# Routing choices packed by expert for each tile of tokens by itself, 32 columns a tile, expert and round

## What is computed

```python
def hierarchical_moe(hn, w_router_group, w_router_expert, w_gate, w_up, w_down):
    g_probs = softmax(t @ w_router_group);  g_w, g_idx = lax.top_k(g_probs, 1)      # 4 groups
    e_in_group = (t @ w_router_expert)[group g_idx]                                  # 8 experts each
    top_l, top_i = lax.top_k(e_in_group, TOP_K_INNER)                                # 2 experts a token
    weights = softmax(top_l) * g_w
    comb = sum(one_hot(ids, N_EXPERTS) * weights[..., None], axis=1)
    for e in range(N_EXPERTS):
        hid = silu(t @ w_gate[e]) * (t @ w_up[e])                                    # 2048 -> 256
        out = out + (hid @ w_down[e]) * comb[:, e:e + 1]                             # 256 -> 2048
```

## Time and profile before

| | before |
|---|---|
| median of 3 runs | 3268.54 us (3267.64 to 3271.41) |
| span of the profiled execution | 3266.3 us |
| PE busy | 2940.1 us, 90% |
| DVE, ACT, POOL busy | 1239.7, 549.1, 697.1 us |
| DMA | 1206.82 MB, 369 GB/s over the span |

### The profile page before, as it was taken

The page is one execution under the profiler, slowest core; times in us unless marked ns, Lnnn a source line. Parts: engine busy times, 40 slices in busy tenths (PEclk is TensorE's granted clock), DMA queues, the critical chain, the costliest instruction groups (busy, mean ns, idle before and its releaser), DMA issues.

```text
span 3266.3 us, 24078 instructions
## 1 busy us (share of the span) xinstructions
PE 2940.1 (90%) x8045; PEld 1303.3 (40%) x8045; DVE 1239.7 (38%) x1913; ACT 549.1 (17%) x1298; POOL 697.1 (21%) x599
## 2 busy tenths in 40 slices
PE   8999998899999999997688788878799899999999
PEld 4444444344444444443333333333354433333344
DVE  1101004535454443345756655554522122322220
ACT  1111001112121110112213211211122111000010
POOL 1000002323234222223434434334300010000000
PEclk9999999999999999998889888998899999999999
DMA  9878888999999999999999999999977659999972
GB/s 358 300 278 288 303 302 311 416 412 412 416 416 419 421 422 421 422 421 416 412 419 406 419 419 419 419 419 419 373 278 262 238 238 422 422 422 422 422 299 78
DMA packets 268084, 1206.82 MB, mean 369 GB/s; under 512 B 16656, under 2 KB 19280, under 8 KB 164688
## 3 DMA queue, kind: packets, MB, share of 16 engines
q1 hardware_dynamic: 193600, 668.09, 52.8%
q0 software_dynamic: 74384, 537.49, 39.8%
HBM read 1203.41 MB, written 2.10 MB: 369 GB/s over the span
## 4 chain that ended last, share of the span: by engine, by line
PE 47%; DMA 40%; DVE 4%; issue 3%; DVEq 2%; ACT 1%; SPq 1%; POOL 1%; ACTq 0%; POOLq 0%
DMA W<-in_peer_expert_down,big 27%; PE bank L973 14%; DMA W<-in_w_expert_up 8%; PE bank L1545 6%; PE bank L963 5%; PE bank L1150 5%; PE bank L1652 4%; DMA W<-in_w_in 4%; PE bank L1710 3%; PE bank L1040 3%; DVEq L2471 2%; DVE W L2622 2%; PE bank L1636 1%; PE bank L1622 1%; DMA W<-in_w_peer_query 1%
## 5 line engine op out<-in xcount | busy, mean ns | idle before, releaser
L2622 DVE CUSTOM_DVE_ANT_0 W<-W,big 128x2048 f32<-128x2048 f32 x256 | 586.3, 2291 | 703.6 <-DMA W<-in_peer_expert_down,big 702.8
L901 POOL DMA_INDIRECT W<-in_peer_expert_down,big x256 | 351.8, 1374 | 1206.8 <-DVE small L2622 643.8
L1545 PE MATMUL bank<-XT,big 128*128 128x512 f32 x488 | 304.5, 782 | 206.8 <-ACT big L2002 186.4
L973 PE MATMUL bank<-W,XT 128*128 128x512 f32 x672 | 297.9, 601 | 5.3 <-DMA W<-in_w_peer_query 5.3
L1545 PEld LDWEIGHTS bank<-XT,big 128*128 128x128 f32 x488 | 119.9, 256 | 381.1 <-issue 258.4
L1545 PE MATMUL bank<-XS,big 128*128 128x512 f32 x536 | 246.3, 603 | 24.0 <-ACT big L2002 18.2
L1994 ACT ACTIVATE small<-small 128x1 f32<-128x1 f32 x256 | 51.8, 202 | 1223.0 <-DVE small L2622 1203.6
L1545 PE MATMUL bank<-W,big 128*128 128x512 f32 x512 | 235.7, 604 | 16.2 <-ACT big L2002 12.9
L1652 PE MATMUL bank<-W,XS 128*64 128x512 f32 x1024 | 226.6, 596 | 14.1 <-DMA W<-in_w_expert_up 11.4
L1150 PE MATMUL bank<-W,XT 128*128 128x512 f32 x480 | 214.9, 598 | 13.4 <-DMA W<-in_w_in 11.6
L963 PE MATMUL bank<-W,XT 128*128 128x512 f32 x480 | 211.4, 598 | 4.1 <-DMA W<-in_w_in 4.1
(11 more groups left out here) (387 smaller groups left out, 2715.4 us busy)
## 6 DMA issues: line engine op xcount, KB each, us to landing
W<-in_w_in SPq DMA_DIRECT2D x66, 2048.0 KB, 7.9
W<-in_w_in SPq DMA_DIRECT2D x132, 1024.0 KB, 12.5
W<-in_w_expert_gate SPq DMA_DIRECT2D x68, 1024.0 KB, 15.0
W<-in_w_expert_up SPq DMA_DIRECT2D x68, 1024.0 KB, 17.0
big<-in_w_expert_down SPq DMA_DIRECT2D x32, 2048.0 KB, 12.6
W<-in_w_out SPq DMA_DIRECT2D x16, 2048.0 KB, 8.1
W<-in_w_out SPq DMA_DIRECT2D x32, 1024.0 KB, 11.6
W<-in_w_peer_query SPq DMA_DIRECT2D x28, 1024.0 KB, 11.4
```

Of the source, the lines that this page charges most:

```text
L901: pool.indirect_dma_start(down_row(n), None, down_t, row).then_inc(down_in[n % DOWN_ROWS], 16)
L973: mm = pe.matmul(out, lhs(k), slot(i)[:, k, :], start=first and k == 0, stop=last and k == ks - 1)
L1545: mm = pe.matmul(bank[4 * (n // P) + c][:, :], DIAG[:, m % 4, :], up_row(n)[:, c * CH:(c + 1) * CH], start=n % P == 0, stop=n % P == P - 2)
L2622: dve.tensor_tensor_reduce(out=down_row(n), in0=down_row(n), in1=HN[n // P], scale=1.0, scalar=0.0, op0=ALU.mult, op1=ALU.add, accum_out=d ...
```

## The change

Each tile's choices are packed on their own: 256 places a tile instead of 512 for both, and 32 columns (CAPT) per tile, expert and round. An expert still has 64 columns in the loop, 32 from each tile. A further round is run if an expert has more than 32 choices in one tile.

The routing code on DVE becomes three functions called once a tile: `choose_experts`, `count_experts`, `place_choices`. For tile 0 they are steps of the table, during tile 1's output projections; for tile 1 they follow `logits(1)`. Tile 0's packing matmuls (`pack(0, ...)`) follow the table on PE, tile 1's follow those. A pair of slices k shares a bank (two times 256 columns); tile 0 uses banks 0 to 2, tile 1 banks 4 to 6. All of tile 0's pairs are moved out by ACT; of tile 1's, ACT takes the odd ones and DVE the even. `keep_scaled(1)` leaves ACT: POOL copies tile 1's columns unscaled, and the scale goes into tile 1's SELP. The index row that SELP is compared with is 256 wide and is loaded earlier. POOL copies 8 windows a pair instead of 4, each half as wide. Cut to its core:

```diff
+CAPT = CAP // T2
+MAX_ROUNDS = P // CAPT
-PACKED = 512
+PACKED = 2 * P
+            put(dve, a + 4, "experts", 0)
+            put(pe, a + 6, "rank", 0)
+            put(dve, a + 7, "places", 0)
 # SP
+            sp.dma_start(places_iota, consts[:, CONST_W:CONST_W + PACKED]).then_inc(iota_loaded, 16)
             for i in range(INDEX["in2", 1, 1, 0], UG):
                 load(i)
-            sp.dma_start(iota512, consts[:, CONST_W:CONST_W + PACKED]).then_inc(iota_loaded, 16)
 # POOL
+            for c in range(4):
+                pool.wait_ge(out2_added, 4 + c + 1)
+                pool.tensor_copy(XS[:, 1, :].rearrange("p (k d) -> p k d", k=KC)[:, :, 32 * c:32 * c + 32],
+                                 H[:, 1, c * CH:(c + 1) * CH].rearrange("p (d k) -> p k d", k=KC)).then_inc(xs_ready, 1)
...
+                        pool.wait_ge(packed_first, KC // 2)
+                        pool.wait_ge(packed_act, 2)
+                        pool.wait_ge(packed_dve, 2)
+                        for e in range(2):
+                            for t in range(T2):
+                                to = e * CAP + t * CAPT
+                                pool.tensor_copy(XTE[:, p, 0:7, to:to + CAPT], XPA[:, t, :, ds(at[e][t], CAPT)])
                         pool.wait_ge(packed_act, 4)
-                        pool.wait_ge(packed_dve, 3)
+                        pool.wait_ge(packed_dve, 4)
...
 # PE
+            def pack(t, pairs):
+                for j in pairs:
+                    if j == 0:
+                        pe.wait_ge(places_ready, t + 1)
+                        pe.wait_ge(xs_ready, 5 if t else 1)
+                        pe.wait_ge(out2_added, 7)
...
+                    if j >= 3 and t == 0:
+                        pe.wait_ge(packed_first, j - 2)
+                    elif j >= 3:
+                        pe.wait_ge(packed_dve if j % 2 else packed_act, (j - 3) // 2 + 1)
+                    for k in (2 * j, 2 * j + 1):
+                        mm = pe.matmul(pack_out(t, k), XS[:, t, k * P:(k + 1) * P], SELP[:, t, :], start=True, stop=True)
+                    mm.then_inc(packed_mm, 1)
+            pack(0, range(0, 5))
+            rank(1)
+            pack(0, range(5, KC // 2))
+            pack(1, range(KC // 2))
 # ACT
-            keep_scaled(1)
-            act.wait_ge(route_in, 1)
+            for j in range(KC // 2):
+                keep_packed(0, j, packed_first)
+            act.wait_ge(route_in, 2)
             act.activation(GEXP, GEXP, ACT.Exp)
             act.activation(RSC[:, :, 0:1], RSC[:, :, 0:1], ACT.Exp).then_inc(route_exp, 1)
-            for k in range(0, KC, 2):
-                act.wait_ge(packed_mm, k + 1)
-                act.activation(packed(k), bank[4 + k % 4][:, :], ACT.Copy, scale=GP[:, k:k + 1]).then_inc(packed_act, 1)
+            for j in range(1, KC // 2, 2):
+                keep_packed(1, j, packed_act)
 # DVE
+                    elif kind == "experts":
+                        dve.wait_ge(attended, 8)
+                        choose_experts(*what)
+                    elif kind == "places":
+                        count_experts(*what)
+                        place_choices(*what)
...
             logits(1)
+            choose_experts(1)
+            count_experts(1)
+            place_choices(1)
...
-                TS(over[:, m - 1:m], most, float(m * CAP), None, ALU.is_gt)
+                TS(over[:, m - 1:m], most, float(m * CAPT), None, ALU.is_gt)
...
-            for k in range(1, KC, 2):
-                dve.wait_ge(packed_mm, k + 1)
-                TS(packed(k), bank[4 + k % 4][:, :], GP[:, k:k + 1], None, ALU.mult).then_inc(packed_dve, 1)
+            for j in range(0, KC // 2, 2):
+                dve.wait_ge(packed_mm, KC // 2 + j + 1)
+                TT(packed_pair(2 * j), bank[4 + j % 3][:, :].rearrange("p (k s) -> p k s", k=2),
+                   GP[:, 2 * j:2 * j + 2].unsqueeze(2).to_broadcast([P, 2, PACKED]), ALU.mult).then_inc(packed_dve, 1)
```

More of the change, by code:

```diff
@@ L620, in half_of, with packed, pack_out, packed_pair @@
             return W[:, half_slot(half, e), :].rearrange("p (g n) -> p g n", g=2)
[L622 to L624 removed]
+        def packed(t, k):
+            return XPA[:, t, k, 0:PACKED] if k < 7 else XPB[:, t, k - 7, 0:PACKED]
+        def pack_out(t, k):
+            return bank[4 * t + k // 2 % 3][:, k % 2 * PACKED:(k % 2 + 1) * PACKED]
+        def packed_pair(k):
+            return XPA[:, 1, k:k + 2, 0:PACKED] if k < 7 else XPB[:, 1, k - 7:k - 5, 0:PACKED]
         def moving(half, e, k):
@@ L1532, in turn3, with rank @@
                 turn_four(turn3_out(t, c), H[:, t, c * CH:(c + 1) * CH]).then_inc(turned3, 1)
+            def rank(t):
+                pe.wait_ge(comb_ready, t + 1)
+                if t == 0:
+                    pe.wait_ge(probs_kept, 8)
+                tri = const("tri")
+                for j in range(2):
+                    mm = pe.matmul(bank[7][:, (2 * t + j) * EXPERTS:(2 * t + j + 1) * EXPERTS], tri[:, j * P:(j + 1) * P],
+                                   PICK[:, t, :], start=True, stop=True)
+                mm.then_inc(ranked, 1)
+            def pack(t, pairs):
[4 more added lines that the diff above has]
+                        pe.wait_ge(out2_added, 7)
+                        if t == 1:
+                            pe.wait_ge(kept3, 8)
+                            pe.wait_ge(logits_ready, 2)
+                    if j >= 3 and t == 0:
[5 more added lines that the diff above has]
+                    mm.then_inc(packed_mm, 1)
             pe.wait_ge(late_rows, 4 * 16)
@@ new lines, in place_choices @@
+            def place_choices(t):
+                one = [SELP[:, t, :], SELQ]
+                dve.wait_ge(iota_loaded, 16)
+                dve.drain()
+                for q in range(2):
+                    if t == 0:
+                        TS(one[q], places_iota, PLACE[:, t, q:q + 1], None, ALU.is_equal)
+                    else:
+                        TS(one[q], places_iota, PLACE[:, t, q:q + 1], rstd[:, t:t + 1], ALU.is_equal, ALU.mult)
+                dve.drain()
+                TT(one[0], one[0], one[1], ALU.add).then_inc(places_ready, 1)
```

204 lines of the change are left out of this document (93 added, 111 removed).

## The result

The changed kernel takes **3243.48 us**, the median of 4 runs (3242.88 to 3247.04). The kernel before, on the same chip, takes 3268.76 us (3267.64 to 3271.41, 4 runs). The ratio is 0.992, with a 95% interval of 0.9908 to 0.9932: faster by 25.3 us. Forecast were 3248 us and a range from 3244 to 3256.

A forecast was written before the change was run, and what follows sets the result against it. The path was held to run from router through packing to the loop's first refill; the loop starting 20.85 us earlier, less 0.45 for tile 0's ranks, gave span 3245.9, plus 2.2 to the median: 3248.1 us, range 3244 to 3256.

The forecast's parts named there:

- what bounds the kernel: Router to expert loop: 44.8 us on the path; an earlier loop start moves the first weight refill and the end.
- Rival 5: Expert loop starts earlier but ends when it did, which needs DMA busy before 2655 us; chance 0.01.
- fewer columns: Packing on PE: the same 64 records with 256 columns take 0.215 us each at full clock, instead of 0.43.
- Rival 2: Packing: each 256-column record waits for its bare weight load; gain 11.4 to 13 us, 3255.5 us or more; chance 0.03.
- tile 0's routing beside the projections: During tile 1's projections: DVE routes tile 0 with 3 us to spare; its ranks cost PE 0.45 us.
- DVE's hold: Tile 1's fourth packing pair: PE stands 2.5 us, a new wait, until DVE's first eviction.
- rival 3: Tile 1's packing: DVE holds PE under 1 us; gain near 22.5 us, 3246 us, or 3244 at full clock; chance 0.05.
- the clock term: Packing: 6 to 11 of the first 20 records at half clock, plus 1.1 us for a renewed fall after DVE's hold.
- the low bound: Whole kernel: the lower end of the predicted range, 3244 us, meant to take in the clock bounds nearly whole and rival 3.
- clock full throughout: Router to loop: DVE counts from 2606.4, later steps come 1.9 us earlier, 1.1 us vanishes; gain 23.4, time 3245.1 us.
- Rival 1: Both packings: low clock stays through most, as two waits cut PE's work; gain 11.4 to 17, 3251 to 3257 us; chance 0.12.
- Rival 4: Expert loop: over 32 choices in one tile makes all 16 pairs run again, adding 459 us, 3707 us; chance 0.02.

The follow-up runs named there:

- Six banks: Changed kernel with six PSUM banks in turn for tile 1's packing instead of three, so PE need not wait for DVE's first eviction: 3246.73 us, ratio 0.9923.
- the repetition: The changed kernel run and profiled once more with nothing changed: 3246.48 us, ratio 0.9924.
- after_filled: Changed kernel with unused matmuls of constants in PE's waits: 3242.77 us, ratio 0.9915.
- tile0_late: Changed kernel with tile 0's choosing, ranks and places moved back behind the table, narrow packing kept: 3259.14 us, ratio 0.9962.

## Why the prediction was right, and where it failed

**Right: what bounds the kernel.** The path was held to run from the router through packing to the first refill, and from there a fixed time to the end. The refill came 24.28 us earlier and the span 24.3 us; the rest of the span differs by 0.6. Rival 5 (nothing gained) falls.

**Right: fewer columns.** At full clock 12 records take 2.86 us and 20 take 4.58, so each further one costs 0.215 us, the value forecast. Every one of them has a weight load of its own, about 0.2 us long:

```profile
2615.98 4.18 PEld L1583 LDWEIGHTS bank<-big,XS 128*128 128x128 f32 x20 [2.37 <-DVE XT L2873]
```

The rule of the Trainium skill (TensorE: Matmul & The Clock Gate, section The mechanism), that a weight load overlaps a matmul only on other rows of the array, would make that near 0.4 us by these rows; the trace disagrees, and the measurement decides. Another section of the same page of the Trainium skill (Step-by-step: what each phase is for) also lets a load into the background weight buffer run ahead, and with that the trace agrees. Rival 2 falls. The narrow packing is worth 12.7 us at full clock.

**Right: tile 0's routing beside the projections.** DVE had 3.87 us left before its next addition, where I expected 3. With the ranks, PE comes from U to the next transposes in 34.78 us instead of 34.33, so they cost 0.45 (forecast 0.45). POOL's scattered copies took 1.05 us each, not 0.6. That costs nothing, since the cover would have held four times 0.6.

**Right: DVE's hold.** It stands ahead of tile 1's fourth pair and ends with DVE's first multiply, as forecast; DVE's work ahead of that took 4.2 us (forecast 4.3). It is 1.96 us long instead of 2.5, and so rival 3 (under 1 us) falls as well. Six banks show it on the path.

**Right on timing of the rest.** ACT's table load begins at 2611.44 and `route_exp` is near 2613.0 (forecast 2613.4), just ahead of DVE's use of it at 2613.07. No wait of DVE for it is seen. PE goes from packing into the loop in 2.9 us (forecast 3.2).

**Wrong: the clock term, and with it the low bound.** The gain in the stretch was forecast as 20.4 us and came as 24.9, 4.5 more. In the time that is 4.6: the rest of the span was 0.6 us longer than before, and the median lay 1.5 us above the profiled span, not 2.2. Piece by piece, with times counted from U:

| step | forecast, us | measured, us | more gained, us |
|---|---|---|---|
| start of packing, from U | 57.0 | 55.7 | 1.3 |
| first 20 records | 6.2 | 6.1 | 0.1 |
| tile 1's count and places | 3.5 | 3.25 | 0.25 |
| tile 1's packing with the hold | 10.5 | 9.4 | 1.1 |
| packing to loop | 3.2 | 2.9 | 0.3 |
| loop's first half | 15.36 | 13.95 | 1.4 |

Three of these are the clock, and that is the step that failed: the forecast carried low clock over from the trace of before, or added it, at three places where after had none. It started packing where the router of before ends, 1.92 us long with slow transposes ahead of it; in after the same eight records take 1.08. It left the loop's first half at 15.36, where 13.95 was measured, and wrote in the Bounds that full clock would be 13.9, without crediting it. And it charged 1.1 us for a renewed fall in the gap of the hold, while the first 20 records were charged as well; in the fourth row that 1.1 is the whole difference, since the hold came 0.5 us shorter and the 32 records 0.5 us longer than forecast. Together that is some 3.7 of the 4.5 us. The last charge was not wrong in kind: a fall behind the hold does occur (6.27 us in the repetition), but in each of three executions it came instead of the first, never with it.

The same omission set the range. The bound "clock full throughout", 3245.1 us, put only the packing at full clock and kept the slow router and the slow loop start of before, 2.6 us. With these credited it would have been 3242.5, and the stretch 105.5 us; `after_filled`, at full clock throughout, has 105.0. So the terms other than the clock were right to 0.5 us in their sum. The range also had nothing for the scatter of everything ahead of U. The same kernel in a later comparison gave 3246.48, inside the range, with a stretch that is equal to 0.01 us.

**Rival 1 (the low clock stays)** falls: one batch of records is slow and no more. But its premise, that new waits keep the clock low, has something to it: in `tile0_late`, with two more waits, 7.0 us of low clock are found where after has 1.7.

**Rival 4 (a second round)** did not occur. Forced, it costs 479 us, 20 more than priced. The step that failed is the reading of the loop's end, near 3105 instead of 3120.3, which is 15 us; the 7.6 us between the rounds were left out as well.

**Left open:** what decides at which place the clock falls in an execution, whether the slow loop start behind six banks was chance, and what bounds the 1.75 us from the last eviction to the loop.

## What to carry to other kernels

Taking a wait away gives its length and also the low clock that stood behind it: here 8.4 us of waiting were worth 13.7, though the 5.3 of clock are read from one execution of each kernel and 0.85 of them lay ahead of the waits. When you price a change that closes gaps, put each slow piece of the old trace, the ones behind the change too, at both levels and let the low bound have them all at the high one. Before pricing a second pass over a loop from its length, follow the last pair to its last matmul, and add the gap between the passes.

## What the runs showed of the hardware

- **The low clock moves between executions of one kernel.** In three executions of the changed kernel the slow batch was the first 20 records once (6.25 and 4.58 us) and the last 20 twice (4.56 and 6.27), with the stretch at 106.6 us each time. In three of the kernel before the stretch went from 130.1 to 131.6. Behind equal waits of 2.6 us the loop of before started at full clock once and slow twice.
- **Unused matmuls in the waits buy time.** Seven to fourteen of them, in waits that PE has anyway, went with a stretch shorter by 1.7 us in after, 4.1 to 5.6 in before (1.2 of it ahead of any filler) and 7.0 in `tile0_late`.
- **A weight load of all 128 rows hides behind a 256-column f32 matmul**: 0.215 us from record to record, with a load of about 0.2 us each.
- **A copy on POOL that gathers 32-column pieces with a large stride** took 1.05 us for 128x512, where 128x576 in runs of 64 columns takes 0.668.
